# Chunk chain of a recurrent layer on 64x64 states, with the queues around it reordered

## Chip, cores and metric

One core of a Trainium2 chip. The metric is the device time of one execution of the whole program in microseconds (us); the time before is the median of three runs.

## What is computed

A decoder layer on 256 tokens of width 2048: RMSNorm, one projection, two head groups side by side (a gated linear recurrence, and RWKV-7 with 16 heads of 64), an output projection, a retrieval layer, and a last norm. The change lies in the RWKV group. Its recurrence, per head, with a 64x64 state:

```
def step(state, inp):
    r_t, w_t, k_t, v_t, na_t, b_t = inp
    sa = einsum("bhij,bhj->bhi", state, na_t)
    state = state * w_t + sa[..., None] * b_t + v_t[..., None] * k_t
    return state, einsum("bhij,bhj->bhi", state, r_t)
...
kk = normalised(k * k_k);  k = k * (1 + (a - 1) * k_a);  b = kk * a;  na = -kk
y = group_norm(y) * lnx_w + lnx_b;  y = (y + bonus) * g
```

## The kernel before

The kernel is written queue by queue: for each engine one function issues its instructions in the order in which they stand, and semaphores order the engines among each other. The first stage runs the input projection as 43 tiles of 128 output columns. A tile is two loads of 512 KB; ScalarE rounds each to fp32r (`hi`, L679), VectorE subtracts (`lo`, L1062), and TensorE makes 48 products of 256 columns from them (`ps<-hT,hi` and `ps<-hT,lo`). `result(t)` then takes a tile out of its bank: a ScalarE copy (`mshift`, `xpad` or `gate`) and for most tiles VectorE work (`rkv`, or four operations on `xc`). Tiles use two banks in turn, so tile t+1 needs tile t-1 out of its bank.

The RWKV group is worked in four groups of four heads (`for g in range(GROUPS)`), each with nine tiles of the projection (seven in the last group) placed into its waits: `m(step)` runs a whole tile at a named step where `ROOM[g]` holds the step. A group goes through these parts:

- The first third: `zw`, `za`, `gate` (low-rank products), a scan `P`, the exponentials `iP` and `P`, the norm `ss`, `kn`, `kb`, then `k`, `kt`, `rk`, `kk`, `bb`, `bt`, `ARt`. Tiles `m(0)` to `m(3)` lie between them. The last group has no tile at steps 0 and 1.
- The scores: `m1`, `m0`, `m3`, `m2` are products of 64x64 blocks, each in two banks by head parity. VectorE masks them into `L1` (m1), `TT` (m0), `Tm` (m3) and `L2` (m2), adds the identity to `Tm` and `TT` (L1275, L1276), and so opens the first inverse.
- Five levels that refine the inverse (`y`, then `t` and `tt`), with small pieces of one tile between them.
- The chunk chain, four chunks of 64 tokens (`for c in range(4)`): the right-hand side `r` from `L2`, the values and the state, copied by ScalarE to `Rm` (L819); `sa` = inverse times `Rm`, copied by VectorE to `SA` (L1304); the state `st` from `Kt` and `Vt`, from the old state by way of the identity, and from `Bt` and `SA`, scaled by VectorE to `ST` (L1308); the output `yc` of two chunks. A state tile is 128x128 and holds two heads on its diagonal blocks; the rest is zeroed by a factor made from `blk` (L1067 on `sq`).
- The rows of y are normed (`unit_rows`), turned by TensorE (`yt`, L2010) and finished on VectorE to `yT`, `yR_hi` and `yR_lo`.

Banks 2 to 7 are given to the RWKV jobs in turn, as they are listed in `RWKV_JOBS`; a job waits until the job before it in its bank has been read.

## Time and profile before

| | us |
|---|---|
| median of 3 runs (2043.71 to 2045.46) | 2044.36 |
| the profiled execution's own time | 2048.04 |
| its span | 2046.2 |
| TensorE busy | 1971.6 (96%) |
| VectorE busy | 1568.9 (77%) |
| ScalarE busy | 963.8 (47%) |

The profile is of one execution. PE is TensorE's matmul, DVE VectorE, ACT ScalarE, POOL GpSimd. Two profiled matmul records stand for one product of f32 by f32 and one for a product of fp32r. All work of TensorE is recorded under the helper's line L1693, so its parts are told apart by the names of what they write and read. Ends of matmuls are modelled, and so a stretch is best measured from one start to the next.

### The profile page before, as it was taken

What the parts mean: (1) busy time and instruction counts of PE and PEld (TensorE: products, weight loads), DVE (VectorE), ACT (ScalarE), POOL (GpSimd) and SP (SyncE); (2) the same over time, 40 slices, a digit from 0 to 9 for tenths busy, and PEclk for the clock granted to TensorE, in tenths of its full rate; (3) what the DMA queues carried; (4) which work ended last, traced back from release to release, by engine and by line L of the source; (5) the groups of instructions that cost most, each with busy time, mean ns of one, the idle gap of its engine ahead of it and who ended that gap; (6) DMA issues with size and microseconds to landing.
All of it is one profiled execution on the core that took longest, in us unless ns stands there. A gap on an engine that the chain in (4) does not pass through costs nothing.

```text
span 2046.2 us, 35624 instructions
## 1 busy us (share of the span) xinstructions
PE 1971.6 (96%) x14176; PEld 1749.5 (85%) x14176; DVE 1568.9 (77%) x2373; ACT 963.8 (47%) x1358; POOL 502.7 (25%) x511
## 2 busy tenths in 40 slices
PE   8999999899999999999999999998899999999997
PEld 7988888787899888888888888888888888888886
DVE  5647474757453799997868888758988999999997
ACT  5434342446353444445444444445664444444444
POOL 0000000000000000000012222104666766667663
PEclk9999999899999999999999999999999999999999
DMA  7524232225565565666578888867879999999996
GB/s 236 181 75 121 68 124 74 83 84 175 185 206 168 183 185 186 186 186 185 188 224 285 279 286 287 272 187 237 284 225 346 348 343 347 346 357 359 356 350 235
DMA packets 149604, 462.02 MB, mean 226 GB/s; under 512 B 19936, under 2 KB 45056, under 8 KB 148928
## 3 DMA queue, kind: packets, MB, share of 16 engines
q1 hardware_dynamic: 115760, 339.49, 51.5%
q0 software_dynamic: 33680, 120.26, 16.6%
q8 instruction: 113, 1.85, 0.4%
q14 instruction: 51, 0.42, 0.1%
HBM read 430.24 MB, written 29.43 MB: 225 GB/s over the span
## 4 chain that ended last, share of the span: by engine, by line
PE 84%; DVE 9%; ACT 2%; issue 2%; DMA 2%; POOL 0%; DVEq 0%; SPq 0%; ACTq 0%; POOLq 0%
PE ps L1693 84%; DVE lo L1062 2%; DVE oneJT L1067 2%; DVE ps L1578 1%; ACT hi L679 1%; DMA raw<-in_w_in 1%; DVE xc L1070 0%; DMA raw<-in_w_out 0%; DMA oneI<-oneI_spill 0%; ACT hT L701 0%; ACT x_sq L874 0%; DMA x_sb<-in_x 0%; DVE L L1259 0%; PE ps L1853 0%; ACT la L851 0%
## 5 line engine op out<-in xcount | busy, mean ns | idle before, releaser
L1693 PE MATMUL ps<-hT,hi 128*128 128x512 f32 (+1 forms) x3936 | 1080.5, 347 | 7.2 <-DVE rkv L1070 5.0
L1693 PE MATMUL ps<-hT,lo 128*128 128x256 f32 x2992 | 842.6, 282 | 0.0
L1693 PEld LDWEIGHTS ps<-hT,hi 128*128 128x128 f32 x3936 | 686.2, 192 | 107.2 <-DVE rkv L1070 6.3
L1062 DVE TENSOR_TENSOR lo<-raw,hi 128x1024 fp32r<-128x1024 f32 x406 | 492.5, 1224 | 227.6 <-ACT hi L679 221.2
L679 ACT ACTIVATE hi<-raw 128x1024 fp32r<-128x1024 f32 x406 | 424.5, 1060 | 443.3 <-DMA raw<-in_peer_u 369.3
L1693 PEld LDWEIGHTS ps<-hT,lo 128*128 128x128 f32 x2992 | 571.3, 191 | 0.0
L637 POOL DMA_INDIRECT got<-in_peer_v,row_ids x256 | 328.8, 1285 | 160.1 <-DVE sums L1070 98.5
L936 ACT ACTIVATE vhi<-vraw 128x1024 fp32r<-128x1024 f32 (+1 forms) x256 | 202.4, 816 | 272.1 <-DMA vraw<-in_peer_v 254.1
L1558 DVE TENSOR_TENSOR vlo<-vraw,vhi 128x1024 fp32r<-128x1024 f32 (+1 forms) x256 | 237.6, 929 | 44.3 <-ACT vhi L936 23.4
L1693 PE MATMUL ps<-vhi,a_hi 128*128 128x512 f32 (+1 forms) x768 | 251.7, 382 | 3.1 <-DVE a_lo L1611 1.6
L1693 PE MATMUL ps<-vlo,a_hi 128*128 128x512 f32 (+1 forms) x768 | 252.5, 383 | 0.0
L1693 PE MATMUL ps<-vhi,a_lo 128*128 128x512 f32 (+1 forms) x768 | 250.4, 381 | 0.0
L1070 DVE SCALAR_TENSOR_TENSOR sums<-got,wT,sums 128x576 f32<-128x576 f32 x256 | 207.7, 812 | 0.2
L1693 PEld LDWEIGHTS ps<-vlo,a_hi 128*128 128x128 f32 x768 | 144.1, 188 | 28.2
L1693 PEld LDWEIGHTS ps<-vhi,a_lo 128*128 128x128 f32 x768 | 144.2, 188 | 24.6
L1693 PEld LDWEIGHTS ps<-vhi,a_hi 128*128 128x128 f32 x768 | 144.1, 188 | 24.2 <-issue 3.6
...
L599 POOL DMA_DIRECT2D oneJ_spill<-madeJ x64 | 34.6, 541 | 206.4 <-DVE madeJ L1534 206.4
L1405 DVE TENSOR_TENSOR Zq<-ps,Zq 128x256 f32<-128x256 f32 x129 | 78.8, 611 | 6.5 <-ACT Zq L904 6.5
L904 ACT ACTIVATE Zq<-ps 128x256 f32<-128x256 f32 x129 | 79.1, 614 | 5.9 <-PE ps L1693 5.5
L1693 PE MATMUL ps<-Zq,oneJT 128*128 128x128 f32 x480 | 64.9, 278 | 12.6 <-DVE oneJT L1067 12.3
...
## 6 DMA issues: line engine op xcount, KB each, us to landing
raw<-in_peer_u SPq DMA_DIRECT2D x256, 512.0 KB, 3.6
vraw<-in_peer_v SPq DMA_DIRECT2D x128, 512.0 KB
...
vraw<-in_peer_v SPq DMA_DIRECT2D x128, 224.0 KB
...
```

What stands on the lines that cost most here:

```text
L599: pool.dma_start(oneJ_dram[g], madeJ[g % 3][:, :, :].rearrange("p t j -> p (t j)")).then_inc(sem(f"oneJ_out{g % 3}"), 16)
L637: pool.indirect_dma_start(out=got[k % N_GATHER][:, :], out_offset=None, in_=v_rows, in_offset=bass.IndirectOffsetOnAxis(ap=row_ids[:, t, e ...
L679: nc.scalar.activation(hi[n % NR][:, :], raw[n % NR][:, :], ACT.Copy).then_inc(hi_done, 1)
L904: nc.scalar.activation(Zq[:, i // 4, part, i % 4], bank("tile", T_U + i)[:, part], ACT.Copy).then_inc(sem("z_in"), 1)
L936: nc.scalar.activation(vhi[i % V_HIS][:, cols_v], vraw[i % V_RAWS][:, cols_v], ACT.Copy).then_inc(hi_done, 1)
L1062: V.tensor_tensor(lo[n % NR][:, :], raw[n % NR][:, :], hi[n % NR][:, :].bitcast(F32), ALU.subtract).then_inc(lo_done, 1)
L1067: V.tensor_scalar(o, i, s1, None, op0)
L1070: return V.scalar_tensor_tensor(out=o, in0=i0, scalar=s, in1=i1, op0=op0, op1=op1)
L1405: V.tensor_tensor(Zq[:, i // 4, part, i % 4], bank("tile", T_U + i)[:, lo_part], Zq[:, i // 4, part, i % 4], ALU.add).then_inc(freed("tile ...
L1558: V.tensor_tensor(vlo[i % V_RAWS][:, cols_v], vraw[i % V_RAWS][:, cols_v], vhi[i % V_HIS][:, cols_v].bitcast(F32), ALU.subtract).then_inc( ...
L1578: V.tensor_tensor(pb, pb, one_i(g)[:, :, :], ALU.mult).then_inc(sem("picks_chosen"), 1)
L1693: return nc.tensor.matmul(o, lhsT, rhs, start=start, stop=stop, skip_group_check=True)
```

## The change

On TensorE, `m2` moves from behind `m3` to behind the products `y1`. The products with a state are made for each head alone, 64x64 in a quadrant of the array, instead of 128 wide for a pair of heads; `r` and `yc` lie in two banks each, by head parity, and the chunk jobs get fixed banks. The products from the values (`from_values`) for the first two chunks no longer wait for the last level's `tt5`, and those for the last two stand in the middle of a tile. Of the last tile of a group six products stand between `sa_3` and the products that wait for `SA`.

On VectorE, `m2`'s masks move behind `y1`'s, the two additions of the identity become one, the factor made from `blk` is gone, `kk`, `aT` and `k` lose five operations, the sum and the centring of `yc` become two operations each, the last tile's `result` moves behind `unit_rows(g, 1)`. On ScalarE, `sq` (a square with a scale) and the factor of `k2` are new, the two `hi` pieces at step 1 stand before the exponentials, the result of that step stays behind them, and a Sqrt of one column is added ahead of `kn`'s. The arithmetic factors (2.0, 0.5, -2.0) make up for `aT` and `kn` that are no longer scaled.

```diff
-             "m1_0", "m1_1", "m0_0", "m0_1", "m3_0", "m3_1", "m2_0", "m2_1"]
+             "m1_0", "m1_1", "m0_0", "m0_1", "m3_0", "m3_1", ]
-    RWKV_JOBS += [f"y{_lv}_0", f"y{_lv}_1"]
+    RWKV_JOBS += [f"y{_lv}_0", f"y{_lv}_1"] + (["m2_0", "m2_1"] if _lv == 1 else [])
-RWKV_JOBS += ["r0", "yc0", "st0", "sa0", "r1", "st1", "sa1", "r2", "yc1", "st2", "sa2", "r3", "sa3"]
+CHUNK_BANKS = {"r0": 5, "r1": 6, "yc0": 7, "yc1": 2, "st": 3, "sa": 4}
...
# ScalarE
+                for c in range(2):
+                    ins = nc.scalar.activation(sq[:, c], rkv[g % 2][:, 1, c], ACT.Square,
+                                               scale=col("k_k", 2 * g + c))
                 m(0)
...
+                    ins = nc.scalar.activation(k2[:, c], aT[:, c], ACT.Identity,
+                                               scale=hka[:, 2 * g + c:2 * g + c + 1],
+                                               bias=oka[:, 2 * g + c:2 * g + c + 1])
...
+                if 1 in ROOM[g]:
+                    his(marks[0])
                 act.wait_ge(sem("scan_done"), g + 1)
...
-                m(1)
+                if 1 in ROOM[g]:
+                    result(marks.pop(0) - 1)
+                nc.scalar.activation(scal[:, 63:64], eps_c, ACT.Sqrt)
...
-                    nc.scalar.activation(Rm[rows, :, :].rearrange("p a b -> p (a b)"),
-                                         bank(f"r{c}", g)[rows, 0:256], ACT.Copy).then_inc(
-                        freed(f"r{c}", g), 1)
+                    for par in range(2):
+                        wait_full(act, f"r{par}_{c}", g)
+                        nc.scalar.activation(Rm[rows, par:4:2, :], bank(f"r{par}_{c}", g)[rows, 0:P].rearrange(
+                            "p (a b) -> p a b", a=2), ACT.Copy).then_inc(freed(f"r{par}_{c}", g), 1)
...
# VectorE
-                for c in range(2):
-                    link(ts(kk[:, c], K[:, c], cg("k_k", c), None, ALU.mult))
-                mark(V.tensor_tensor(sq[:, :, :], kk[:, :, :], kk[:, :, :], ALU.mult), "sq_done", g + 1)
...
-                wait_read(dve, "za", g)
-                link(ts(aT[:, :, :], aT[:, :, :], 0.5, 0.5, ALU.mult, ALU.add))
-                for c in range(2):
-                    link(ts(k2[:, c], aT[:, c], cg("k_a", c), oka[:, 2 * g + c:2 * g + c + 1],
-                            ALU.mult, ALU.add))
+                dve.wait_ge(sem("k2_factor"), g + 1)
...
-                        pcm = sq[:, c % 2].rearrange("p (c q) -> p c q", c=2)
-                        for ct in range(2):
-                            k = 4 * ct + c
-                            link(ts(pcm[:, ct], blk, P65[:, k, 64:65], None, ALU.mult))
...
-                    m(6 + c)
+                    if c < 3:
+                        m(6 + c)
                     if c == 2:
                         unit_rows(g, 0)
+                los(marks[0])
                 unit_rows(g, 1)
                 dve.sem_inc(sem("y_rows_done"), 1)
+                result(marks.pop(0) - 1)
...
# TensorE
+                oy = from_values(0)
                 for c in range(4):
...
+                    if c:
+                        o = [job(f"r{par}_{c}") if c != 2 else bank(f"r{par}_{c}", g) for par in range(2)]
+                        wait_read(pe, f"st_{c - 1}", g)
+                        for hl in range(4):
+                            ct, par = hl // 2, hl % 2
+                            mine = half_rows(par)
+                            ins = mm(o[par][turned, place(hl)], ARt[mine, 0, ct, tok], ST[c % 2][mine, ct],
+                                     False, hl >= 2)
+                            mm(oy[par][rows, place(hl)], ARt[mine, 1, ct, tok], ST[c % 2][mine, ct],
+                               False, False)
+                    if c < 3:
+                        o = job(f"st_{c}")
+                        for ct in range(2):
+                            for par in range(2):
+                                mm(o[half_rows(par), CHUNK * ct:CHUNK * ct + CHUNK],
+                                   Kt[rows, ct, t, CHUNK * par:CHUNK * par + CHUNK],
+                                   Vt[rows, ct, t, CHUNK * par:CHUNK * par + CHUNK], ct == 0, False)
+                        if c:
+                            mm(o[:, 0:P], ident[:, :], ST[c % 2][:, :, :].rearrange("p c q -> p (c q)"),
+                               False, False)
+                    osa = job(f"sa_{c}")
+                    if c == 0:
+                        for half in range(2):
+                            wait_read(pe, f"tt5_{half}", g)
...
+                    if c < 3:
+                        m(6 + c, (0,))
+                    else:
+                        tile_part(marks[0], 0, 0, 2)
+                    wait_read(pe, f"sa_{c}", g)
...
+                    if c == 1:
+                        tile_part(marks[0], 1, 0, 4)
+                        oy = from_values(1)
+                        tile_part(marks.pop(0), 1, 4, 8)
+                    elif c < 3:
+                        m(6 + c, (1,))
+                    else:
+                        tile_part(marks[0], 0, 2, 8)
+                        tile_part(marks[0], 1, 0, 8)
```

How the order moves is shown at three places, all in the first group. Numbers behind a name tell buffers of one name apart (`k_96` is `k2`, `ST_111` one of two states, `L_109` is `L1`, `L_110` is `L2`). First TensorE, from the scores to the first level of the inverse, with the rows of the tile left out, and of `y1` the second pair; before:

```order
L1693 MATMUL ps<-ARt,bt 64x128 x16
L1693 MATMUL ps<-ARt,bt 64x64 x16
L1693 MATMUL ps<-bt,ARt 64x64 x16
L1693 MATMUL ps<-ARt,kt 64x128 x16
...
L1693 MATMUL ps<-idcb,identb 64x256 x2
L1693 MATMUL ps<-Tm,L_109 64x64 x8
```

and now:

```order
L1713 MATMUL ps<-ARt,bt 64x128 x16
L1713 MATMUL ps<-ARt,bt 64x64 x16
L1713 MATMUL ps<-bt,ARt 64x64 x16
...
L1713 MATMUL ps<-idcb,identb 64x256 x2
L1713 MATMUL ps<-TmTT,L_109 64x64 x8
L1713 MATMUL ps<-ARt,kt 64x128 x16
```

The 16 products `ARt,kt` are m2; the half tile that stood behind them (at "...") now follows `bt,ARt` directly.

Second TensorE in the chunk chain, from the last level into chunk 1, before:

```order
L1693 MATMUL ps<-Vt,L_110 64x64 x16
L1693 MATMUL ps<-Vt,Kt 128x128 x2
L1693 MATMUL ps<-Rm,TT 64x64 x4
...
L1693 MATMUL ps<-SA,Bt 128x128 x2
...
L1693 MATMUL ps<-ST_111,ARt 64x128 x4
L1693 MATMUL ps<-Vt,Kt 128x128 x2
L1693 MATMUL ps<-ST_111,ident 128x256
L1693 MATMUL ps<-Rm,TT 64x64 x4
```

and now:

```order
L1713 MATMUL ps<-Vt,L_110 64x64 x16
L1713 MATMUL ps<-Vt,Kt 64x64 x4
L1713 MATMUL ps<-Rm,TmTT 64x64 x4
...
L1713 MATMUL ps<-SA,Bt 64x64 x4
...
L1713 MATMUL ps<-ST_111,ARt 64x64 x8
L1713 MATMUL ps<-Vt,Kt 64x64 x4
L1713 MATMUL ps<-ST_111,ident 128x128
L1713 MATMUL ps<-Rm,TmTT 64x64 x4
```

There are more products, each a quarter as large or less, and the order among the kinds is kept.

Third ScalarE in the first third of the first group, before:

```order
L785 ACTIVATE gT<-ps 128x512
L789 ACTIVATE iP<-P_100 128x512
L793 ACTIVATE P_100<-P_100 128x520
L679 ACTIVATE hi_61<-raw_51 128x1024
L679 ACTIVATE hi_62<-raw_52 128x1024
L737 ACTIVATE mshift_74<-ps,cols 128x256
L797 ACT_TABLE_LOAD
L797 ACTIVATE kn<-ps 128x8
```

and now:

```order
L794 ACTIVATE k_96<-aT,idxT 128x256 x2
L799 ACTIVATE gT<-ps 128x512
L677 ACTIVATE hi_61<-raw_51 128x1024
L677 ACTIVATE hi_62<-raw_52 128x1024
L805 ACTIVATE iP<-P_100 128x512
L809 ACTIVATE P_100<-P_100 128x520
L735 ACTIVATE mshift_74<-ps,cols 128x256
L813 ACT_TABLE_LOAD
```

The pair of `hi` moved ahead of `iP`, and the factor of `k2` (two operations) came in ahead of both.

## Rows read from the trace of the kernel before

**Rows 1.** The page: busy time, share of the span and instructions of each engine.
```profile
PE 1971.6 (96%) x14176; PEld 1749.5 (85%) x14176; DVE 1568.9 (77%) x2373; ACT 963.8 (47%) x1358; POOL 502.7 (25%) x511
```
**Rows 2.** Windows: length, busy us of PE, PEld, DVE, ACT, POOL, granted clock, DMA.
```profile
84.00:461.00 377.00, 348.23 (x4854) 318.48 (x4853) 229.59 (x402) 153.48 (x257) 0.00 (x0) 0.96 0.31 92
461.00:2046.20 1585.20, 1549.76 (x8748) 1358.82 (x8746) 1292.24 (x1881) 767.04 (x1034) 495.52 (x497) 1.00 0.77 258
```
**Rows 3.** Waits of PE over the span: us in total, times, longest.
```profile
PE ps L1693 <- DVE L L1259: 9.6, 4, 2.5
PE ps L1693 <- DVE rkv L1070: 5.0, 8, 1.8
PE ps L1693 <- ACT TT L813: 3.1, 4, 0.8
```
**Rows 4.** Windows in stretches of one granted clock.
```profile
109.75:113.05 3.30, 3.30 (x30) 2.97 (x23) 2.29 (x5) 0.00 (x0) 0.00 (x0) 0.50 0.02 5
...
399.90:403.15 3.25, 3.25 (x18) 3.25 (x17) 1.54 (x3) 0.00 (x0) 0.00 (x0) 0.50 0.00 0
...
226.00:262.00 36.00, 34.44 (x450) 30.54 (x446) 15.76 (x31) 13.29 (x23) 0.00 (x0) 1.00 0.32 92
```
**Rows 5.** Timeline of PE, second group, scores: start, length, what, idle before.
```profile
205.69 0.65 PE L1693 MATMUL ps<-bt,ARt 64*64 64x64 f32 x32
208.81 1.99 PE L1693 MATMUL ps<-ARt,kt 64*64 64x128 f32 x32 [2.47 <-DVE L L1259]
...
214.38 0.30 PE L1693 MATMUL ps<-idcb,identb 64*64 64x256 bf16 x2
```
**Rows 6.** Timeline of DVE, the same place.
```profile
205.53 0.69 DVE L1259 TENSOR_TENSOR L<-ps,masks 128x512 f32<-128x512 f32 x1 [1.67 <-PE ps L1693]
...
207.97 0.69 DVE L1259 TENSOR_TENSOR L<-ps,masks 128x512 f32<-128x512 f32 x1
```
**Rows 7.** Timeline of PE, second group, last level into chunk 0.
```profile
231.60 0.69 PE L1693 MATMUL ps<-Vt,L 64*64 64x64 f32 x32 [0.79 <-ACT TT L813]
232.22 0.71 PE L1693 MATMUL ps<-Vt,Kt 64*128 64x128 f32 x4
232.86 0.68 PE L1693 MATMUL ps<-Rm,TT 64*64 64x64 f32 x8
233.47 0.39 PE L1693 MATMUL ps<-hT,hi 128*128 128x256 f32 x1
```
**Rows 8.** Timeline of PE, second group, chunk 1.
```profile
240.24 0.66 PE L1693 MATMUL ps<-ST,ARt 128*64 128x128 f32 x8
240.83 0.71 PE L1693 MATMUL ps<-Vt,Kt 64*128 64x128 f32 x4
241.47 0.70 PE L1693 MATMUL ps<-ST,ident 128*128 128x256 f32 x2
242.10 0.68 PE L1693 MATMUL ps<-Rm,TT 64*64 64x64 f32 x8
...
245.77 0.71 PE L1693 MATMUL ps<-SA,Bt 64*128 64x128 f32 x4
```
**Rows 9.** Timeline, first group, chunk 3 and what follows.
```profile
161.50 0.65 PE L1693 MATMUL ps<-Rm,TT 64*64 64x64 f32 x8 [0.54 <-ACT Rm L819]
...
163.29 0.68 PE L1693 MATMUL ps<-SA,L 64*64 64x64 f32 x16 [1.15 <-DVE SA L1304]
163.91 0.39 PE L1693 MATMUL ps<-hT,hi 128*128 128x256 f32 x1
...
171.60 0.48 PE L1693 MATMUL ps<-hT,hi 128*128 128x256 f32 x2
```
**Rows 10.** Timeline, second group, the wait in the first third.
```profile
186.06 2.36 DVE L1062 TENSOR_TENSOR lo<-raw,hi 128x1024 fp32r<-128x1024 f32 x2 [2.38 <-ACT hi L679]
...
186.81 0.45 ACT L737 ACTIVATE mshift<-ps,cols 128x256 f32<-128x256 f32 x1
...
188.87 0.50 PE L1693 MATMUL ps<-hT,hi 128*128 128x256 f32 x2 [1.76 <-DVE rkv L1070]
```

201 lines of the change are left out of this document (102 added, 99 removed).

## The prediction

> **What bounds the kernel now.** I read the page first: TensorE is busy 96% of the span [rows 1], so a change counts only if it takes products, waits or slow clock from TensorE. The windows by stage come next: the RWKV stretch from 84 to 461 us has the most slack, 348 of 377 us busy at a mean granted clock of 0.96, while behind it TensorE is busy 1550 of 1585 us at 1.00 [rows 2]. The change touches only that stretch, and all that follows hangs on its end, so I carry every microsecond through to the end one for one. The list of TensorE's waits names three that the change aims at: four waits for the mask of `L` (9.6 us), eight for `rkv` (5.0), four for `TT` (3.1) [rows 3]. The granted clock shows the rest. Eight stretches of 3.4 us, two for each group, run at half speed, 1.2 instead of 2.4 GHz (0.50, first and last of them in [rows 4]); each costs half its length, 1.7 us. Four follow the wait for the mask of `L`, three the waits at chunk 3 of a group, one a wait of the last group for `sq`. In the chunk chain itself the clock is 1.00 (226 to 262 us, [rows 4]).
>
> **a. m2 behind y1.** Today TensorE ends m3 at 206.2, waits 2.5 us until VectorE has read `m1_1` and its bank is free, does m2, half a tile at partly half clock, and starts `y1` at 214.38: 8.69 us from m3's start [rows 5]. Now m3 (0.57) and the half tile (24 products, 3.0 us at the pace of [rows 7, 8], where 24 lie in the 3.07 us between a `Rm,TT` and a `SA,Bt`) follow each other; y1 starts 3.57 us after m3. Its second half needs the first inverse of both parities. VectorE starts its masks at 205.53, and one parity takes 2.44 us (207.97 minus 205.53, [rows 6]), 2.36 with the two additions in one of 0.69 instead of 0.42+0.42. So the inverse is ready at 205.53+4.72 = 210.25, 4.6 us after m3's start; y1's first half ends at 4.2: a wait of 0.5. y1 itself costs what it did. m2 comes behind it and now covers the mask of y1: 16 products, at the 0.03 of four quadrants (c) and twice as wide, so 0.9 and 0.15 for the change. In place of 8.69 us there are 3.57+0.5+1.05 = 5.12: 3.57 less, 14.3 in four groups. 1.6 of each is the slow stretch, which goes because a wait of 0.5 takes the place of 2.5. Bounds: if the new wait is 0 or 1 us, 12 to 16.
>
> **b. Values ahead of tt5.** The products `Vt,L` wait 0.79 us for ScalarE's copy [rows 7]. They and `Vt,Kt` don't need it and now cover it: 0.8 a group, 3.2 in all. The chunk jobs' new banks are those of the last level; `st` needs `tt5_0`, which is read before `Vt,L` ends.
>
> **c. Products in quadrants.** Starts in [rows 7, 8] give the price now: `Vt,L` 0.62 for 16 products in four quadrants (0.03 each and 0.15 at the change of kind), `Vt,Kt` 0.64 for 2, `Rm,TT` 0.61 for 4 in one quadrant (0.115 each and 0.15), `ST,ARt` 0.59 for 4, `ST,ident` 0.63, `SA,Bt` the same 0.71 of length as `Vt,Kt`. `SA,L`, 8 products in two quadrants in turn, takes 0.62 from start to start [rows 9]: 0.058 each and 0.15. After the change: `ST,ARt` is 8 products in four quadrants, 0.23; `Vt,Kt` and `SA,Bt` are 4 products in two quadrants, 0.23; `ident` is half as wide, 0.42 with the change. The 0.15 falls away where two kinds of the same shape now meet. No run shows two quadrants that share their rows without the other two in play, so their bounds are 0.03 (the row of four quadrants) and 0.115 each (one quadrant); I take 0.058, the row with as many quadrants.
> Chunk 0: `Vt,L`+`Vt,Kt` 1.26 to 0.85, `SA,Bt` 0.64 to 0.38, and a new wait of 0.2, since only 0.23 now cover the copy of `Rm`: 0.47 less. Chunk 1: 2.47 to 1.64, and `SA,Bt`+`SA,L` 1.26 to 0.85: 1.24 less; `Rm` is read 1.2 us after the first `ST,ARt` (its length of 0.66 [rows 8] and the 0.54 of [rows 9]); with two copies I take 1.05 and 1.27, and the products of the two parities are due at 1.03 and 1.26, so there is no wait. Chunk 2: the same without `SA,L`, 1.09 less, and 0.15 more for the tile cut in two: 0.95. Sum 2.66 a group, 10.6 in all. What VectorE saves here (the factor from `blk`, twice 0.3 a chunk) is worth nothing: 3 us of tile cover it. Bounds 5 and 13.
>
> **d. Chunk 3 and the hand-over.** TensorE waits for `Rm` (0.54) and for `SA` (1.15 in the first group, where VectorE is in the convolution of a tile, [rows 9]). In the first and third group VectorE has the same queue ahead of `SA`, so the products `SA,L` start no earlier; in the others `r` in two copies gains 0.2 and the six products of the tile cost it. The gain is that these six (0.73) are then done. From the end of `SA,L` to the next group's first tile it is 7.69 us now (163.91 to 171.60), with a slow stretch in it. After: 42 products 5.1, the rows of y ready at 5.5 (VectorE: sums and centring 2.3, two `lo` 2.4 as in [rows 10], rows 0.65), turning 0.4: 5.95. 1.7 less, three times: 5.1. Of this 1.4 is the clock, which I expect to hold, as 0.6 of the waits is filled by the tile; if it falls all the same, this term is about 1.5. The last group gains 0.2: its rows are ready sooner, but the convolution that `lru_gates` needs now stands behind them.
>
> **e. The first third.** Step 2's tile waits 1.76 us for `rkv` [rows 10]: `lo` waited 2.38 for `hi`, and `rkv` stands behind two `lo` (2.36). With `hi` ahead of the exponentials the `lo` end before `mshift`. But ScalarE now has 0.75 more for the factor of `k2` and 0.7 for the squares; `mshift` ends 0.7 later and `rkv` ends 0.35 earlier than now. Behind it VectorE has 1.4 us less work (three operations of `aT` and `k`), but `kn` comes 0.6 later; about 0.3 is left. Group 1 gains 0.9, group 2 0.6. In group 3 the convolution moved behind `unit_rows` delays `yT`, then `hi`, and ScalarE also loads two tables: I work out 1.1 more. Group 4 has no tile to delay at steps 0 and 1, and `sq` comes from ScalarE at once: 0.8 less. Sum 1.2; bounds -6 (if ScalarE's queue sets each step) and 4.
>
> **Sum.** 14.3 + 3.2 + 10.6 + 5.1 + 0.2 + 1.2 = 34.6 us less. The profiled execution took 2048.0 us (span 2046.2), 3.7 above the median, so it would become 2013.4; taken from the median, 2044.4 becomes **2009.8**.
>
> **Rivals.** 1. *Quadrants with the same rows run one after the other.* Then each of the four products of `Vt,Kt` and `SA,Bt` costs what a product of `Rm,TT` does: 0.61 for four, no less than now. Terms: 1.86 a group of c go, 7.4 in all: 2017.2. For it: nothing but `Rm,TT` shares rows and no other quadrant. Against: the 16 of `Vt,L` reach 0.03, which they could not with one quadrant of each row half at a time. The Trainium skill ("TensorE: Matmul & The Clock Gate", What overlaps and what doesn't) says that a weight load overlaps running products only where the row group differs, which is the rule for this rival; the trace of before has no such pair alone. Chance 0.12.
> 2. *ScalarE takes the first third.* Squares, factor and table loads hold `hi` and `mshift` back in every group; d and e come to -0.5 together instead of 6.5: 2016.8. For it: `lo` already waits on `hi` [rows 10]. Chance 0.16.
> 3. *The clock goes to half in the chunk chain, and it is slower than before.* More of TensorE's time there is short products in one quadrant or two, and waits of 0.2 to 0.5 stand among them. Each stretch of 3.4 us costs 1.7 us, so 20 more than now eat the 34.6. From `Vt,L` to the hand-over a group is 30 us, nine stretches; if all 36 run at 1.2 GHz it costs 61 us: 2071. Against: today's chain, with waits of the same size, holds 1.00 [rows 4]. Chance 0.05, of which 0.02 end within 0.2% of before and 0.03 slower.
> 4. *More than that.* No wait is left in d and e but TensorE's own work: 6 us more, 2004. Chance 0.07.
> The forecast keeps 0.60.
>
> **Numbers.** 0.2% of 2044 is 4.1 us, about what a measurement tells. Rivals 1, 2 and 4 are all faster: faster 0.95, same 0.02, slower 0.03. The forecast's own terms spread by 4 us for a and c and 3 for d; with rivals 1 and 2 above and 4 below the range is 2002 to 2020. What is outside is rival 3 and the sum of several bounds.
>
> **What would show it.** `ARt,kt` stands behind the y1 products and no wait for a mask of `L` over 0.7 us is left; no half clock near the scores. `Vt,L` starts within 0.2 us of `tt5`. `Vt,Kt` to `Rm,TT` takes 0.23 to 0.3 in chunk 0, `ST,ARt` to `Rm,TT` 1.0 in chunk 1. From `SA,L`'s end to the next group 6 us. Wrong would be: 0.46 for `Vt,Kt` (rival 1), a wait for `rkv` or `lo` of 2 us or more in every group (rival 2), clock below 0.97 between 84 and 430 us (rival 3).

## The result, and the profile after

The changed kernel took **2012.62 us** (median of 4 runs, 2012.10 to 2014.07) where the kernel before took 2044.03 in the same session: a ratio of 0.9846, 95% interval 0.9829 to 0.9863, so 28 to 35 us faster. Forecast were 2009.8 us in a range of 2002 to 2020. The profiled executions were 2048.0 us before and 2012.1 us after, 35.9 us apart; the one before was 4 us above its median, the one after was not. The page of the changed kernel, its busy times (as [rows 1]):

```profile
PE 1952.9 (97%) x14368; PEld 1735.6 (86%) x14368; DVE 1549.9 (77%) x2338; ACT 974.3 (48%) x1394; POOL 503.0 (25%) x511
```

The windows after, as [rows 2, 4] (length, busy us of PE, PEld, DVE, ACT, POOL, granted clock, DMA):

```profile
84.00:427.00 343.00, 330.51 (x5053) 305.07 (x5052) 215.44 (x372) 160.29 (x291) 0.00 (x0) 0.99 0.34 103
427.00:2010.30 1583.30, 1549.67 (x8740) 1359.05 (x8738) 1288.94 (x1879) 769.49 (x1034) 495.81 (x497) 1.00 0.77 258
268.90:272.20 3.30, 3.30 (x17) 3.30 (x17) 3.12 (x8) 3.11 (x4) 0.00 (x0) 0.50 0.00 0
...
357.70:360.95 3.25, 3.25 (x16) 3.25 (x16) 3.11 (x7) 0.94 (x2) 0.00 (x0) 0.50 0.00 0
```

The whole gain lies in the RWKV stretch; behind it TensorE has the same 1549.7 us of work as before. Of the eight half-clock stretches there three are left (first and last shown), all in the third and fourth group's first third. None stands behind the scores or at a hand-over any more. The waits of PE over the span, as [rows 3]:

```profile
PE ps L1713 <- DVE lo L1080: 6.4, 5, 2.4
PE ps L1713 <- DVE rkv L1088: 3.9, 5, 1.7
PE ps L1713 <- ACT Rm L838: 2.0, 5, 0.4
```

The waits for the mask of `L` (9.6 us) and for the copy of `TT` (3.1) are gone from the list, those for `rkv` fell from 5.0 to 3.9 only, and those for `lo` rose from 4.7 to 6.4. Timeline of PE, second group, scores, as [rows 5] (start, length, what, idle before):

```profile
194.59 0.65 PE L1713 MATMUL ps<-bt,ARt 64*64 64x64 f32 x32
...
198.22 0.30 PE L1713 MATMUL ps<-idcb,identb 64*64 64x256 bf16 x2
...
199.19 0.30 PE L1713 MATMUL ps<-idcb,identb 64*64 64x256 bf16 x2 [0.20 <-DVE TmTT L1292]
...
199.78 1.04 PE L1713 MATMUL ps<-ARt,kt 64*64 64x128 f32 x29
```

From m3 to y1 it is 3.63 us (forecast 3.57), the new wait for the first inverse is 0.20 (forecast 0.5), and `ARt,kt` stands behind it. The same engine in chunk 0 and, further down, in chunk 1 of that group, as [rows 7, 8]:

```profile
215.73 0.69 PE L1713 MATMUL ps<-Vt,L 64*64 64x64 f32 x32
216.22 0.43 PE L1713 MATMUL ps<-Vt,Kt 64*64 64x64 f32 x8
216.89 0.67 PE L1713 MATMUL ps<-Rm,TmTT 64*64 64x64 f32 x8 [0.25 <-ACT Rm L838]
...
224.01 0.46 PE L1713 MATMUL ps<-ST,ARt 64*64 64x64 f32 x16
224.31 0.40 PE L1713 MATMUL ps<-Vt,Kt 64*64 64x64 f32 x8
224.64 0.49 PE L1713 MATMUL ps<-ST,ident 128*128 128x128 f32 x2
225.06 0.68 PE L1713 MATMUL ps<-Rm,TmTT 64*64 64x64 f32 x8
```

`ST,ARt` to `Rm,TmTT` in chunk 1 takes 1.05 us where it took 1.86, and `Vt,Kt` 0.33 where it took 0.64. The value products no longer wait. First group, chunk 3 and the hand-over, as [rows 9]:

```profile
152.91 0.65 PE L1713 MATMUL ps<-Rm,TmTT 64*64 64x64 f32 x8 [0.43 <-ACT Rm L838]
...
154.89 0.68 PE L1713 MATMUL ps<-SA,L 64*64 64x64 f32 x16 [0.43 <-DVE SA L1315]
155.50 0.51 PE L1713 MATMUL ps<-hT,hi 128*128 128x256 f32 x2
...
160.76 0.63 PE L2057 MATMUL ps<-ident,y_tm 128*128 128x128 f32 x4
161.15 0.48 PE L1713 MATMUL ps<-hT,hi 128*128 128x256 f32 x2
```

From the end of `SA,L` to the next group's first tile it is 5.65 us, before 7.69. What got worse is the first third of the third group. There ScalarE has this queue, then VectorE and TensorE wait (as [rows 10], which is the second group):

```profile
260.78 1.09 ACT L794 ACTIVATE k<-aT,idxT 128x256 f32<-128x256 f32 x2
261.78 0.58 ACT L799 ACTIVATE gT<-ps 128x512 f32<-128x512 f32 x1
262.25 2.00 ACT L677 ACTIVATE hi<-raw 128x1024 fp32r<-128x1024 f32 x2
264.27 1.28 ACT L805 ACT_TABLE_LOAD   x1
265.56 0.63 ACT L805 ACTIVATE iP<-P 128x512 f32<-128x512 f32 x1
266.22 0.64 ACT L809 ACTIVATE P<-P 128x520 f32<-128x520 f32 x1
266.77 0.46 ACT L735 ACTIVATE mshift<-ps,cols 128x256 f32<-128x256 f32 x1
```
```profile
265.19 0.95 PE L1713 MATMUL ps<-blk,sq 128*128 128x2 f32 x8
267.80 0.51 PE L1713 MATMUL ps<-hT,hi 128*128 128x256 f32 x2 [1.65 <-DVE rkv L1088]
```

`mshift` is last in a row of 6.4 us; its tile was complete on TensorE by 265.2. A half-clock stretch follows the wait (268.90, above). How much is wait and how much is clock can be read from the windows of the first thirds of groups 3 and 4 (length, then TensorE's busy time; the difference is its waits), before:

```profile
270.35:303.63 33.28, 32.29 (x309) 30.60 (x311) 25.35 (x39) 19.54 (x28) 0.00 (x0) 1.00 0.47 145
368.81:395.62 26.81, 22.57 (x212) 20.40 (x214) 21.53 (x36) 15.28 (x23) 0.00 (x0) 0.94 0.34 102
```

and now:

```profile
249.82:285.43 35.61, 33.80 (x307) 31.96 (x310) 24.77 (x38) 21.17 (x33) 0.00 (x0) 0.95 0.44 136
341.07:368.50 27.43, 23.95 (x211) 22.00 (x214) 18.69 (x31) 16.43 (x27) 0.00 (x0) 0.88 0.31 97
```

Group 3 waits 1.8 us instead of 1.0 and is busy 1.5 us longer with the same products, which is its half-clock stretch. Group 4 waits 3.5 instead of 4.2 and is busy 1.4 longer: it has two such stretches where it had one.

Put together from the starts in the two traces, in us, the groups counted 1 to 4 as in the prediction:

| term (all are products of TensorE) | group 1 | group 2 | group 3 | group 4 | sum | forecast |
|---|---|---|---|---|---|---|
| a. m3 to the first product with `Ym` | -3.81 | -3.79 | -3.78 | -3.58 | -15.0 | -14.3 |
| b. from there to `Vt,L` | -0.96 | -0.98 | -0.92 | -1.76 | -4.6 | -3.2 |
| c. `Vt,L` to chunk 3's first `ST,ARt` | -2.65 | -2.50 | -2.66 | -2.65 | -10.5 | -10.6 |
| d. from there to the turning of y, in group 4 to `xc,wai`, the first product of `lru_gates` | -2.21 | -2.16 | -2.19 | -0.39 | -7.0 | -5.3 |
| e. first third, to m3 | -0.89 | -0.61 | +2.34 | +0.62 | +1.5 | -1.2 |

The sum is -35.5 against the forecast -34.6, and the two executions end 35.9 us apart: what was gained stands to the end of the program.

### The profile page after: what moved, and what is told of

Read it like the earlier page. It is cut to its first block, busy times and chain, and to the rows that moved or that the text cites. A ratio compares the mean times of both kernels' runs of the same rounds, so it can differ in the third digit from the quotient of the medians.

```text
span 2010.3 us, 36028 instructions
## 1 busy us (share of the span) xinstructions
PE 1952.9 (97%) x14368; PEld 1735.6 (86%) x14368; DVE 1549.9 (77%) x2338; ACT 974.3 (48%) x1394; POOL 503.0 (25%) x511
## 4 chain that ended last, share of the span: by engine, by line
PE 85%; DVE 7%; ACT 3%; DMA 2%; issue 2%; POOL 0%; DVEq 0%; SPq 0%; ACTq 0%; POOLq 0%
PE ps L1713 84%; DVE lo L1080 1%; DVE oneJT L1085 1%; DMA oneI<-oneI_spill 1%; DVE ps L1598 1%; ACT hi L677 1%; DMA raw<-in_w_in 1%; DMA raw<-in_w_out 0%; DVE hT L1088 0%; DVE xc L1088 0%; DVE TmTT L1292 0%; DVE L L1275 0%; DVE lr L1387 0%; PE ps L1873 0%; DMA x_sb<-in_x 0%
## 5 line engine op out<-in xcount | busy, mean ns | idle before, releaser
L597 POOL DMA_DIRECT2D oneJ_spill<-madeJ x64 | 34.6, 540 | 206.0 <-DVE madeJ L1554 206.0
```

What stands on the lines that cost most here:

```text
L597: pool.dma_start(oneJ_dram[g], madeJ[g % 3][:, :, :].rearrange("p t j -> p (t j)")).then_inc(sem(f"oneJ_out{g % 3}"), 16)
```

## Experiments

Two measures are given for each run: the median with its ratio to the kernel before on the same chip (its medians there were 2045 to 2049 us, and 2044.03 for the changed kernel), and, for parts of a few us, the RWKV stretch in the profiled execution, from the first product of the first group (`lora,wa`) to the last group's turning of y. It is 381.88 us before and 344.79 after. The second is one execution, with the half-clock stretches that this execution had; so a part of it can be clock, as the third table below shows.

| kernel | median us | ratio to before, 95% interval | RWKV stretch us |
|---|---|---|---|
| changed kernel | 2012.62 | 0.9846 (0.9829 to 0.9863) | 344.79 |
| only_m2 | 2034.68 | 0.9928 (0.9912 to 0.9945) | 367.10 |
| chunk_only | 2027.94 | 0.9894 (0.9877 to 0.9910) | 358.90 |
| third_only | 2047.87 | 1.0009 (0.9998 to 1.0019) | 375.60 |
| no_m2 | 2025.76 | 0.9873 (0.9849 to 0.9897) | 358.36 |
| old_third | 2015.01 | 0.9830 (0.9810 to 0.9850) | 345.09 |
| conv_back | 2014.31 | 0.9842 (0.9821 to 0.9863) | 346.65 |
| mshift_first | 2012.53 | 0.9837 (0.9816 to 0.9858) | 343.74 |
| sq_early | 2010.61 | 0.9823 (0.9803 to 0.9843) | 341.08 |
| factor_late | 2007.84 | 0.9811 (0.9795 to 0.9827) | 340.95 |
| same_columns | 2015.85 (one run) | | 345.21 |
| handover_plan | 2002.46 | 0.9784 (0.9771 to 0.9797) | 334.80 |
| handover_plan2 | 2002.04 | 0.9781 (0.9766 to 0.9796) | 333.72 |

And the length of the first third, from the turning of y of the group before (in group 1 from `lora,wa`) to m3:

| kernel | group 1 | group 2 | group 3 | group 4 |
|---|---|---|---|---|
| before | 27.17 | 34.44 | 33.27 | 26.81 |
| third_only | 26.28 | 33.78 | 33.26 | 27.29 |
| chunk_only | 27.15 | 35.28 | 33.90 | 26.81 |
| changed kernel | 26.28 | 33.83 | 35.61 | 27.43 |
| old_third | 27.16 | 35.30 | 33.90 | 26.82 |
| mshift_first | 26.27 | 33.81 | 34.55 | 27.43 |
| sq_early | 26.28 | 33.01 | 33.72 | 26.49 |
| factor_late | 25.58 | 32.77 | 33.49 | 27.11 |
| handover_plan | 25.59 | 31.89 | 31.88 | 23.44 |
| handover_plan2 | 25.59 | 31.89 | 31.88 | 21.93 |

What TensorE waits in these first thirds (length minus busy time, from the windows of each), and the half-clock stretches that lie in them, each of which makes TensorE's busy time 1.2 to 1.7 us longer:

| kernel | groups 1 to 4 | sum | stretches, by group |
|---|---|---|---|
| before | 1.2, 2.2, 1.0, 4.2 | 8.6 | one: 4 |
| third_only | 0.3, 1.5, 1.0, 3.5 | 6.2 | two: 4, 4 |
| chunk_only | 1.2, 1.8, 1.6, 4.2 | 8.8 | two: 2, 4 |
| changed kernel | 0.3, 1.5, 1.8, 3.5 | 7.1 | three: 3, 4, 4 |
| old_third | 1.2, 1.8, 1.6, 3.1 | 7.6 | three: 2, 4, 4 |
| conv_back | 0.3, 1.5, 1.0, 3.5 | 6.2 | two: 4, 4 |
| mshift_first | 0.3, 1.5, 2.0, 4.9 | 8.6 | one: 4 |
| sq_early | 0.3, 0.7, 1.4, 4.3 | 6.7 | one: 4 |
| factor_late | 0.0, 0.5, 0.9, 3.3 | 4.6 | two: 4, 4 |
| handover_plan | 0.0, 0.0, 0.0, 2.6 | 2.6 | none |
| handover_plan2 | 0.0, 0.0, 0.0, 1.3 | 1.3 | none |

**only_m2**: the kernel before with `m2` moved behind y1 on TensorE and on VectorE.
```diff
@@ TensorE
-                scores("m2", 2, ...)
                 mid = marks.pop(0)
...
                         done(ins, f"y{lv}_{half}")
+                    if lv == 1:
+                        scores("m2", 2, ...)
```


> The kernel before with one part of the change: the m2 products and their masks stand behind the y1 products, everything else as before. My theory (term a: the wait of 2.5 us for the read of m1_1 and the half-clock stretch behind it go, because 24 tile products and y1 stand where m2 stood): m3 to the first Y product falls from 10.5 to about 6.8 us in each group, no half clock near the scores, and 14 to 15 us less in all: 2029 to 2030 us. Rival (the gain of a needs the joined addition of the identity, or is only the queue ahead of it moved): a wait for the first inverse of 0.8 us and more takes its place, 2 us a group or less come off, 2036 us or more. Second rival (the wait goes but the clock falls all the same, for chunk 3 sets it): 1.7 us a group less than my theory, 2036 us.

Measured: 2034.68 us. The number alone is nearer to the rivals' 2036, but the kernel before took 2049.28 on that chip, and by the ratio it is 14.7 us less (11 to 18). In the trace every group loses 3.65 to 3.68 us between m3 and the first product with `Ym`, 14.6 in all, and no half clock is left near the scores. So term a stands by itself, without the joined addition. A second thing showed: at the hand-over from the second group to the third this execution stayed at full clock, which before did not (its row is 263.40 to 266.60 at 0.50). Timeline of PE there:

```profile
256.58 0.68 PE L1694 MATMUL ps<-SA,L 64*64 64x64 f32 x16 [0.59 <-DVE SA L1305]
...
262.92 0.28 PE L1694 MATMUL ps<-hT,lo 128*128 128x256 f32 x1
264.33 0.63 PE L2012 MATMUL ps<-ident,y_tm 128*128 128x128 f32 x4 [1.13 <-DVEq L1329]
```

TensorE came to the last product of the tile 1.5 us sooner (counted from `SA,L`) and then waited 1.13 us for the rows of y (DVEq is VectorE's queue). `SA,L` to the turning is 7.75 us at full clock and was 7.97 at half. At this hand-over the slow clock had cost 0.2 us, not 1.7.

**no_m2**: the changed kernel with that edit undone.

```diff
+                scores("m2", 2, ...)
                 mid = marks.pop(0)
...
-                    if lv == 1:
-                        scores("m2", 2, ...)
```


> The changed kernel with the m2 products and masks back ahead of the tile (that part alone undone). If the parts add up: the 2.5 us wait and the half clock behind the scores are back in every group, m3 to the first Y product about 10.5 us, and 15 us more than the changed kernel: 2027 us. If the parts cover for each other (without m2 there the other parts would have taken a share of the same wait): less than 12 us more, 2024 us or below.

Measured: 2025.76 us. One of the four runs took 2017.86, and the ratio's interval is wide: it overlaps that of the changed kernel, so the size rests on the trace. There the stretch is 13.6 us longer: 2.2 in the first group, 3.6 to 3.8 in the others. In the first group the wait of 2.4 us is back, but no slow stretch follows it. So the parts add up but for that stretch; they don't cover for each other.

**chunk_only**: the kernel before with the value products ahead of the last level, the quadrants, the two banks, and the new hand-over.
```diff
-RWKV_JOBS += ["r0", "yc0", "st0", "sa0", "r1", "st1", "sa1", "r2", "yc1", "st2", "sa2", "r3", "sa3"]
+RWKV_CHUNKS = [("r0", 0), ("r1", 0), ("yc0", 0), ("yc1", 0), ("st", 0), ("sa", 0), ...
...
+                oy = from_values(0)
...
-                unit_rows(g, 1)
+                los(marks[0])
+                unit_rows(g, 1)
                 dve.sem_inc(sem("y_rows_done"), 1)
+                result(marks.pop(0) - 1)
```


> The kernel before with the chunk chain of the change alone: values ahead of the last level, products in quadrants, two banks by head parity, the tile's last piece and the convolution moved behind chunk 3; m2 and the first third stand as before. My theory (terms b, c, d: 0.8 to 1.0 and 2.65 a group and 2.1 at three hand-overs): 20 us less than before, 2024 us; the chain from the first value product to the last product of chunk 3 is 2.65 us shorter in each group, and the clock from there to the next group's first tile is 1.00. Rival (the clock at the hand-over holds only because the shorter first third or m2 changed what the chip did before): the slow stretches at the hand-overs remain, 1.7 us each, 2029 us.

Measured: 2027.94 us, by the ratio 21.7 us less (18 to 25). The chain from `Vt,L` to chunk 3 is shorter by 2.42 to 2.65 us in each group, every hand-over is at full clock and 2.1 us shorter from `SA,L` to the turning. The median is near the rival's 2029, but the kernel before was 5 us slower there than in the first session, and what tells the two apart, the clock at the hand-overs, is as my theory has it. It also lost 0.84 and 0.63 us in the first thirds of groups 2 and 3, with nothing edited there: in group 3 it is wait (1.6 instead of 1.0), in group 2 a half-clock stretch, while the waits fell (1.8 instead of 2.2). Its first group has the wait that the change removes, and a full clock behind it; timeline of PE:

```profile
110.23 1.10 PE L1702 MATMUL ps<-ARt,kt 64*64 64x128 f32 x32 [2.39 <-DVE L L1265]
111.27 0.51 PE L1702 MATMUL ps<-hT,hi 128*128 128x256 f32 x2
```

Before, the same wait of 2.5 us had 1.2 GHz behind it ([rows 4]) and the 32 products took 1.99 us ([rows 5], second group) instead of 1.10.

**old_third**: the changed kernel with both engines' first third as before.
```diff
-                    ins = nc.scalar.activation(sq[:, c], rkv[g % 2][:, 1, c], ACT.Square, ...
-                    ins = nc.scalar.activation(k2[:, c], aT[:, c], ACT.Identity, ...
-                    his(marks[0])
...
+                    link(ts(kk[:, c], K[:, c], cg("k_k", c), None, ALU.mult))
+                link(ts(aT[:, :, :], aT[:, :, :], 0.5, 0.5, ALU.mult, ALU.add))
```


> The changed kernel with the first third back as before on both engines: squares, factor of k2 and table load leave ScalarE, hi goes back behind the exponentials. I forecast that this part gains 1.2 us; the trace of the changed kernel says that it loses 1.5 to 2. If ScalarE's longer queue is what loses it (rival 2 in small): this kernel is 0 to 3 us faster than the changed one, 2010 to 2012 us, groups 3 and 4 gain about 2 and 1 us and groups 1 and 2 lose 0.9 and 0.6. If instead the new hand-over (the convolution behind the unit rows, a start of the group 2 us earlier) is what loses it, then the old first third loses too, and more: 2013 us or over, with waits for rkv of 2 us and over in groups 2 and 3.

Measured: 2015.01 us (2011.67 to 2018.23), no difference that the ratios tell; the stretch is 0.3 us longer. Groups 1 and 2 lose 0.88 and 1.47, groups 3 and 4 gain 1.71 and 0.61. So in the changed kernel the whole first-third edit is worth nothing in its own part (the four add up to 0.0). Groups 1, 3 and 4 move as the first theory says; group 2 lost 0.9 more than it says, with a half-clock stretch that it didn't have.

**third_only**: the kernel before with that edit alone.

```diff
+                    ins = nc.scalar.activation(sq[:, c], rkv[g % 2][:, 1, c], ACT.Square, ...
+                    ins = nc.scalar.activation(k2[:, c], aT[:, c], ACT.Identity, ...
+                    his(marks[0])
...
-                    link(ts(kk[:, c], K[:, c], cg("k_k", c), None, ALU.mult))
-                link(ts(aT[:, :, :], aT[:, :, :], 0.5, 0.5, ALU.mult, ALU.add))
```


> The kernel before with the first third of the change alone: squares, factor of k2 and hi on ScalarE as in the change, fewer operations on VectorE, the hand-over, m2 and the chunk chain as before. My step e said 0.9 less in the first group, 0.6 in the second, 0.8 in the last, and only the new hand-over made the third 1.1 worse; by that this kernel is 2 to 3 us less than before. The pair of runs with and without it on the changed kernel gave 0.3 us less. Theory A (the part is worth little by itself, since ScalarE's added 1.9 us stand ahead of mshift and kn wherever it is): 0 to 1 us less, with a wait for rkv of 1 us or more in groups 2 and 3. Theory B (it is the new hand-over that spoils it): 2 to 3 us less.

Measured: 2047.87 us against 2046.06, ratio 1.0009: nothing. In its trace the first thirds change by -0.89, -0.66, -0.01 and +0.48, which is -1.1; most of the remaining 5 us of its shorter stretch is a clock that stayed at 2.4 GHz where that of before fell (five half-clock stretches in the place of eight), which the medians don't bear out. In waits it is theory B: 2.3 us less, by group 0.9, 0.6, 0.0 and 0.8, as term e had it. But the last group has a second half-clock stretch behind its wait for `lo` of 2.4 us, which takes 1.2 back. The medians show no gain either, and the mean granted clocks on record go with that: 0.989 in the median of its ten executions, 0.991 in that of the fifteen of the kernel before beside them, each stretch being 0.0008 (3.41 us at half, in 2046). Together with chunk_only the first thirds should make +0.4 and make +1.5; of the 1.1 between, 0.6 is wait.

**conv_back**: in the changed kernel VectorE's convolution ahead of the rows of y again.
```diff
                 los(marks[0])
+                result(marks.pop(0) - 1)
                 unit_rows(g, 1)
                 dve.sem_inc(sem("y_rows_done"), 1)
-                result(marks.pop(0) - 1)
```


> The changed kernel with one thing undone on VectorE: the convolution of the group's last tile stands again ahead of the rows of y of chunks 2 and 3, and so ahead of what TensorE turns at the hand-over. The run with m2 alone moved showed a hand-over at full clock in which TensorE ended the tile's products 1.4 us sooner and then waited 1.4 us for the rows of y. Theory A (VectorE's rows of y set the hand-over, the slow clock there was hidden behind them): the wait for the rows is back, 1.0 to 1.4 us at each of the three hand-overs and the last, the product SA,L to the turning of y grows from 5.87 to about 7.2 us, and since yT and with it hi come sooner behind the turning, 0.6 to 1 us of it is given back in groups 2 and 3: 2 to 3 us slower in all, 2015 us. Theory B (as I forecast: the clock was 1.4 of the 1.7 us): no more than 0.3 us is lost at a hand-over, and with what yT gains it is even or faster, 2010 to 2013 us.

Measured: 2014.31 us. VectorE at the second hand-over:

```profile
251.04 0.41 DVE L1084 TENSOR_SCALAR xc<-xpad,cols 128x256 f32<-128x256 f32 x1
251.49 1.53 DVE L1088 SCALAR_TENSOR_TENSOR xc<-xpad,cols,xc 128x256 f32<-128x256 f32 x3
253.05 0.18 DVE L1207 RECIPROCAL gsd<-gsd 128x4 f32<-128x4 f32 x1
```
```profile
253.89 0.63 PE L2057 MATMUL ps<-ident,y_tm 128*128 128x128 f32 x4 [1.98 <-DVEq L1348]
```

Neither theory as I put it. The wait is there, 2.0 us, but behind the even groups (2 and 4) alone: in groups 1 and 3 the tile in question is a `gate`, for which VectorE has nothing to do, and `SA,L` to the turning stays 5.87. And what it costs at the second hand-over, the third group's first third gives back: 35.61 becomes 33.26, 0.8 of it wait and 1.5 the half-clock stretch that isn't there. In the last group it costs 2.0 to the turning and 0.9 to `lru_gates`. So the place of this convolution is worth little by itself; in the middle it moves 2 us from one side of the turning to the other, and the ratios show no difference.

**mshift_first**, **sq_early**, **factor_late**: in the changed kernel one step moved on ScalarE each: `mshift` ahead of the exponentials; the squares of the next group ahead of the wait for y; the factor of `k2` behind `kn`.
```diff
@@ mshift_first
                 if 1 in ROOM[g]:
                     his(marks[0])
+                    result(marks.pop(0) - 1)
@@ sq_early
+                if g < GROUPS - 1:
+                    squares_of(g + 1)
                 act.wait_ge(sem("y_f32"), g + 1)
@@ factor_late
                     freed("ss", g), 1)
+                wait_read(act, "za", g)
+                for c in range(2):
+                    ins = nc.scalar.activation(k2[:, c], aT[:, c], ACT.Identity, ...
                 m(2)
```


> The changed kernel with one step moved on ScalarE: mshift of the tile of step 1 stands ahead of the two exponentials iP and P instead of behind them. In the trace of the changed kernel the chain in group 3 is exponential table load 1.28, iP, P, mshift at 266.77, rkv, and TensorE's tile waits 1.9 us for it with a half-clock stretch of 3.4 us behind. Theory A (ScalarE's queue holds rkv, so the tile): mshift starts 1.5 to 2.5 us sooner, the waits for rkv of 1.6 and 1.9 us in groups 2 and 3 fall under 0.5 us, the exponentials come 0.7 us later, which nothing of TensorE's waits for: 3 to 5 us faster, 2008 to 2010 us. Theory B (the exponentials feed kt and bt, whose products are next to be late): the wait goes over to the score products or rk, and less than 1 us is gained.

> The changed kernel with the squares of the next group's keys placed on ScalarE ahead of its wait for the rows of y at the hand-over, where it stands idle, instead of behind the turned y. Theory A: the wait for ss of 1.5 us in the last group goes, hi of the tile comes 0.9 us sooner in groups 2 and 3, and 2 to 3 us less in all: 2010 us. Theory B (the rows of the keys come from VectorE too late to square them there, so that ScalarE waits in order and y itself gets late): the turned y comes later, lo with it, and it is 1 us or more slower than the changed kernel.

> The changed kernel with one step moved on ScalarE: the factor of k2 (two operations, 1.1 us) stands behind kn instead of ahead of gT, hi, the exponentials and mshift. Theory A (ScalarE's queue ahead of mshift is what TensorE waits for, and the factor is the part of it that the change put there): the waits for rkv of 1.6 and 1.9 us in groups 2 and 3 fall by 1.1 each, the half clock behind the second goes, kn comes 1.1 sooner in the last group: 3 to 5 us less than the changed kernel, 2008 to 2010 us. Theory B (VectorE's queue behind it takes the time back, as when mshift alone was moved, which gave about 1 us): the wait goes over to the lo of step 2 and less than 1.5 us is gained.

Measured: 2012.53, 2010.61 and 2007.84 us; the stretches are 1.05, 3.71 and 3.84 us shorter. With `mshift` first the wait for the tile of step 1 goes in the third group (in the second 1.20 of 1.34 are left, there `rkv` stands behind two `lo`), and in its place the next tile of the third group waits 1.74 us: `kn` comes 18.8 us after the turning as before, and VectorE's `rk` and `lo` behind it. In the last group a wait of 1.37 us opens behind `kn`. TensorE's waits in the first thirds are 1.5 us more in all, and the shorter stretch comes from two half-clock stretches less: theory B, and no gain in the median. The first row below is the wait in group 3, each row from the PE timeline of its own kernel:

```profile
275.85 0.51 PE L1712 MATMUL ps<-hT,hi 128*128 128x256 f32 x2 [1.74 <-DVE rkv L1087]
```
```profile
267.60 0.50 PE L1718 MATMUL ps<-hT,hi 128*128 128x256 f32 x2 [1.27 <-DVE rkv L1093]
```
```profile
266.50 0.50 PE L1713 MATMUL ps<-hT,hi 128*128 128x256 f32 x2 [0.53 <-DVE rkv L1088]
```

With the squares early (second row) the wait in group 3 falls from 1.65 to 1.27 and that for the squares in the last group goes, but a wait of 1.9 us behind `kn` takes its place there. Three of the groups are 0.8 to 1.9 shorter; of the 3.7 us only 0.4 is wait and the rest clock, the median is 2.0 less, and its interval overlaps that of the changed kernel. So theory A's waits came in part, and its gain is not shown. With the factor late (third row) the wait in group 3 falls to 0.53 and no half clock follows; the waits of the first thirds are 2.5 us less in all, the median 4.8, its interval just clear of that of the changed kernel. That is theory A. Taking the factor out of ScalarE's queue ahead of `mshift` helps; moving `mshift` in front of the exponentials does not.

**same_columns**: the four products of `Vt,Kt` and `SA,Bt` with the two of one quadrant behind each other.
```diff
-                        for ct in range(2):
-                            for par in range(2):
+                        for par in range(2):
+                            for ct in range(2):
```


> The changed kernel with the four products of Vt,Kt and of SA,Bt in another order: the two of the same quadrant follow each other, where now the two quadrants take turns; nothing else. If two products overlap because they are in different columns of the array (what 0.058 us each instead of 0.115 for one quadrant suggests), two of the four now follow in the same quadrant and cost 0.115: Vt,Kt goes from 0.33 to about 0.42 us, and 24 such sets make 2 us more. If instead the pace of 0.058 is that of any product of this size once r and y are not in play, nothing changes, 0.33 us and within 0.5 us in all.

Measured: `Vt,Kt` to `ST,ident` is 0.38 us (0.33 in the changed kernel), the stretch 0.4 us longer. Timeline of PE, second group, chunk 2:

```profile
236.15 0.45 PE L1713 MATMUL ps<-Vt,Kt 64*64 64x64 f32 x8
236.53 0.49 PE L1713 MATMUL ps<-ST,ident 128*128 128x128 f32 x2
```

The order costs 0.05 us a set of `Vt,Kt`, half of what I expected, and from `Vt,L` to chunk 3 the four groups are 0.7 us longer, which is twelve such sets; the `SA,Bt` sets show nothing. Two quadrants of the same rows overlap, and they do so nearly as well when not strictly in turn. The mechanism stays open.

**handover_plan**: the changed kernel with both queues written anew around the hand-over.
```diff
@@ ScalarE
                     result(marks.pop(0) - 1)
+                nc.scalar.activation(scal[:, 63:64], eps_c, ACT.Exp)
                 act.wait_ge(sem("w65_ready"), g + 1)
...
-                    ins = nc.scalar.activation(k2[:, c], aT[:, c], ACT.Identity, ...
                 wait_full(act, "gate", g)
...
                     freed("ss", g), 1)
+                    ins = nc.scalar.activation(k2[:, c], aT[:, c], ACT.Identity, ...
...
+                    squares_of(g + 1)
+                    his(MARKS[g + 1][0])
                 act.wait_ge(sem("y_f32"), g + 1)
@@ VectorE
+                mark(V.memset(w65[:, :, 0:1], 0.0), "w65_ready", g + 1)
                 m(0)
...
                 m(1)
+                if g == GROUPS - 1:
+                    los(marks[0])
...
                 dve.sem_inc(sem("y_rows_done"), 1)
-                result(marks.pop(0) - 1)
+                before_last = marks.pop(0) - 1
+                if g == GROUPS - 1:
+                    result(before_last)
...
                 mark(V.tensor_tensor(yT[:, :, :], yT[:, :, :], gT[:, :, :], ALU.mult), "y_f32", g + 1)
+                    if 0 in ROOM[g + 1]:
+                        los(MARKS[g + 1][0])
+                    result(before_last)
```


> The changed kernel, with the queues of ScalarE and VectorE written for the idle time that its trace shows at the hand-over: squares of the next group and hi of its first tile stand ahead of the wait for y on ScalarE; VectorE does the two lo of that tile behind y and the convolution behind them, in the last group the two lo behind the scan; the factor of k2 stands behind kn, the exponential table is loaded by a small operation ahead of the wait for zw, and the memset that w waits for stands ahead of the tile. Theory A (the first third is set by these two queues, and TensorE's waits of 0.5 to 2.65 us there end with them): against the changed kernel the waits for ss and rkv fall under 0.5 us (1.6 us less in group 2, 1.9 to 2.5 in group 3, 1.5 and 1.0 in the last), the wait for lo of 2.65 us in the last group goes with its half-clock stretch (2.6 to 3.5), 7 to 9 us in all: 2004 to 2006 us. Theory B (the waits pass on to kb, rk and the scores, because VectorE's work behind kn, 10.6 us from kn to ARt and two lo, is what is long): 3 to 5 us, 2008 to 2010 us.

Measured: **2002.46 us**, ratio 0.9784 to the kernel before, its interval clear of that of the changed kernel; the stretch is 10.0 us shorter. ScalarE at the second hand-over:

```profile
245.09 0.90 ACT L766 ACTIVATE sq<-rkv,cols 128x256 f32<-128x256 f32 x2
245.89 1.05 ACT L677 ACTIVATE hi<-raw 128x1024 fp32r<-128x1024 f32 x1
248.91 1.06 ACT L677 ACTIVATE hi<-raw 128x1024 fp32r<-128x1024 f32 x1 [1.98 <-DMA raw<-in_w_in]
251.15 0.63 ACT L860 ACTIVATE yR_hi<-yT 128x512 fp32r<-128x512 f32 x1 [1.18 <-DVE yT L1378]
...
253.50 1.28 ACT L783 ACT_TABLE_LOAD   x1
...
256.30 0.84 ACT L788 ACTIVATE w<-ps,scal 128x256 f32<-128x256 f32 x2 [1.31 <-DVE w L1239]
```

Here the changed kernel had ScalarE idle for 7.25 us ahead of `yR_hi`. Now 3 us of work lie in that time, and the table load of the exponentials lies in a wait. The RWKV stretch in the windows of this kernel, then the longest wait left in its first thirds:

```profile
84.00:416.00 332.00, 323.76 (x5050) 299.39 (x5048) 214.14 (x369) 160.83 (x293) 0.00 (x0) 1.00 0.34 105
```
```profile
PE ps L1739 <- DVE sq L1256: 1.5, 1, 1.5
```

The clock is 1.00 over the whole stretch, with no half-clock stretch left in it. Groups 2, 3 and 4 gain 1.9, 3.7 and 4.0 us in their first thirds. Of the 10.4 us there, 4.5 are waits (7.1 became 2.6), and most of the rest is the three half-clock stretches. That is theory A, 1 us beyond its range. It is faster than both kernels, in the medians too.

**handover_plan2**: that kernel with two steps moved in the last group.
```diff
@@ ScalarE
                     his(MARKS[g + 1][0])
+                if g == GROUPS - 2:
+                    nc.scalar.activation(scal[:, 63:64], eps_c, ACT.Exp)
@@ VectorE
-                m(3)
+                if g < GROUPS - 1:
+                    m(3)
...
                                        Vv.rearrange("p c t -> p (c t)"), ALU.mult), "bsum", g)
+                if g == GROUPS - 1:
+                    m(3)
```


> The kernel with the queues written for the hand-over, with two steps moved in the last group: the exponential table is loaded ahead of the wait for y on ScalarE, and bon stands ahead of the two lo of step 3 on VectorE. Its trace shows two waits of TensorE left there, 1.8 us for kn behind the table load and 1.3 us for bon behind two lo. Theory A (each is set by what stands ahead of it): the first falls to 0.5 and the second to 0, 2 to 2.6 us less in all, 2000 us. Theory B (the lo of step 3 or the scan is next to be late): less than 1 us, 2002 us.

Measured: 2002.04 us, the same. The first third of the last group is 1.5 us shorter, since the wait for `bon` (1.04) went and that behind `kn` fell from 1.54 to 1.31 only. But with `bon` ahead the two `lo` stand directly before VectorE's masks, and a wait for the first inverse opens where there was one of 0.2 at most:

```profile
364.06 0.30 PE L1745 MATMUL ps<-idcb,identb 64*64 64x256 bf16 x2 [1.10 <-DVE TmTT L1318]
```

Theory B. VectorE has no idle time there from `rk` to the masks, so I take it that it bounds the last group and that only work taken from it would help; that was not tried.

## Why the prediction was right, and where it was not

**a, m2 behind y1: right, with its size.** 15.0 us against 14.3; 3.8 a group, because the wait for the inverse was 0.2 and not 0.5. Shown alone by only_m2 (14.7 by the ratio, 14.6 in the trace) and undone by no_m2. One part of its working was too sure: that a slow stretch of 1.7 us goes in every group. A wait of 2.4 us had none behind it in the first group of three kernels (chunk_only, no_m2, third_only), in third_only not in groups 3 and 4 either, and undoing the move in the first group cost 2.2 us and not 3.8.

**b, values ahead of tt5: right, 4.6 against 3.2.** In three groups it is 0.92 to 0.98 each. The last group has 0.8 more, a wait of 0.55 and what hung on it in the levels, which went too; it also went in third_only, where nothing of b was edited, so this 0.8 is not shown to be b's.

**c, quadrants: right, 10.5 against 10.6.** The price that no row of before had, 0.058 a product for two quadrants that share their rows, was what it came to: 0.33 for four products with the change of kind. Rival 1 had 0.61 here and is refuted by the rows of chunk 1. (Its own sum was too high: by the sign that I gave for it, 0.46 for the four products against 0.23, six sets are 1.4 us a group and not 1.86.) The Trainium skill ("TensorE: Matmul & The Clock Gate", What overlaps and what doesn't) has the weight load overlap running products only where the row group differs; the trace does not bear that out for these products, which share their rows and start in pairs 0.006 us apart.

**d, chunk 3 and the hand-over: the size about right (6.6 against 5.1 at the three hand-overs), half of the reason wrong.** I put 1.4 of the 1.7 us of each to the clock. For the hand-overs behind groups 1 and 3 that can stand: no rows of y were waited for, and with 2.4 GHz and six products done ahead it is 2.1 us shorter (no run has the old order at full clock there). Behind group 2 it does not. There the slow clock lay over a wait for the rows of y (only_m2: 7.75 at full clock, 7.97 at half), and what shortened it was VectorE's convolution, moved behind the rows (conv_back: 2.0 back without it). The last group gained 0.4 before `lru_gates`, as I had said of the convolution that they need (0.2).

**e, the first third: the step that failed, +1.5 instead of -1.2.** Its account of the queues was good: TensorE's waits changed by -0.9, -0.6, +0.8 and -0.8 us in the four groups, 1.5 less in all, where I had 0.9, 0.6 and 0.8 less and 1.1 more. What it left out is the clock. Terms a and d count half-clock stretches, and in this one I took it for granted that their number stays; instead a stretch stands behind the wait of 1.65 us in group 3 (+1.5), and a second one behind the wait of 2.4 us for `lo` in group 4 (+1.4). These 2.9 us turn the term round. The stretch of group 3 is there in all three traces with that wait (the changed kernel, no_m2, same_columns), and not in conv_back, where the wait is 0.8 us, nor in factor_late, where it is 0.5.

The wait of group 3 has the cause that I gave: ScalarE's queue (factor of `k2`, `gT`, two `hi`, a table load, two exponentials) ends 2.0 us behind the tile that needs `mshift`, and it starts late because `yT` does. In group 4 the sum was right and its parts were not: the squares don't come at once but behind `yR_hi`, so a wait of 1.1 us is left of 2.7, and that for `lo` grew from 1.1 to 2.4. The runs show the parts alone: the edit of the first third takes 2.3 us of waits away (third_only) and the new chunk chain and hand-over add 0.2 (chunk_only), and each brings one half-clock stretch. Rival 2, ScalarE's queue in every group, did not come: the waits grew in group 3 alone.

**Rival 3** did not come. No half clock fell between `Vt,L` and chunk 3 in any of the profiled kernels. **Rival 4**, 2004 us, needed the waits of the first third gone; handover_plan took most of them away, and the half clock with them, and came to 2002.

**The total.** Trace against trace it was 35.9 us where I had 34.6. That they are so near is in part luck: a, b and d brought 3.8 us more than I had, and e 2.7 less. The median fell by 31.4, because the profiled execution of before was 4 us above its median, and that of the changed kernel was not. I had subtracted the same sum from the median of before, and so was 2.8 us too low. What that execution had more than its median is not on record; two or three half-clock stretches would be about that much, and my sum had seven of its eight in it, at 1.4 to 1.6 us each, as if every execution had them.
